# Single-core transformer stack: uniform widths in runs of full-precision products, rearranged last norm, and 18 added products in the feed-forward blocks

## What is computed

```python
def second_block(x, ...):
    h = x
    for l in range(DEPTH_2):                      # DEPTH_2 is 1
        h = h + 0.5 * swiglu(rmsnorm_2(h, ffn1_norm[l]), ffn1_w_gate[l], ffn1_w_up[l], ffn1_w_down[l])
        n = rmsnorm_2(h, mix_norm[l])
        ...                                       # block attention, spatial gating, sigmoid gates
        h = h + merged @ w_out[l]
        h = h + 0.5 * swiglu(rmsnorm_2(h, ffn2_norm[l]), ffn2_w_gate[l], ffn2_w_up[l], ffn2_w_down[l])
    return rmsnorm_2(h, final_norm)
```

## Time and profile before

| | |
|---|---|
| median of 3 runs | 1138.66 us (1137.09 to 1138.79) |
| profiled execution, its own time | 1136.31 us |
| its span in the profile | 1134.5 us |
| granted TensorE clock, mean | 0.998 |
| PE busy | 1120.8 us, 99% of the span |
| DVE / ACT / POOL busy | 733.8 / 653.8 / 750.8 us |
| chain that ended last, PE's share | 96% |

### The profile page before, as it was taken

How to read it: one execution, slowest core, us unless ns; L and a number is a source line. 1 busy time by engine, 2 the same in 40 slices (tenths; PEclk the granted TensorE clock), 3 DMA queues, 4 the chain that set the end, 5 groups by cost and what they waited for, 6 DMA issues and landing times.

```text
span 1134.5 us, 22331 instructions
## 1 busy us (share of the span) xinstructions
PE 1120.8 (99%) x8968; PEld 1066.2 (94%) x8968; DVE 733.8 (65%) x1261; ACT 653.8 (58%) x1089; POOL 750.8 (66%) x578
## 2 busy tenths in 40 slices
PE   9999999999999999999999999999999999999996
PEld 7788998999988799899999999999899999999996
DVE  6896644566588775265847666667669567666664
ACT  7676854575567577346646444446566447444443
POOL 6787697657488868865764656556865774646552
PEclk9999999999999999999999999999999999999999
DMA  9554354556555534545566566655644655566551
GB/s 319 181 179 130 119 182 151 171 161 205 168 168 169 168 120 151 184 139 180 169 215 202 188 221 188 198 179 178 207 148 131 205 188 166 189 217 191 192 180 38
DMA packets 63895, 199.49 MB, mean 176 GB/s; under 512 B 6992, under 2 KB 17968, under 8 KB 63792
## 3 DMA queue, kind: packets, MB, share of 16 engines
q1 hardware_dynamic: 61920, 194.99, 53.2%
q10 hardware_dynamic: 1872, 3.08, 0.8%
HBM read 196.21 MB, written 1.84 MB: 175 GB/s over the span
## 4 chain that ended last, share of the span: by engine, by line
PE 96%; DMA 1%; DVE 1%; issue 0%; ACT 0%; SPq 0%; DVEq 0%
PE ps L1665 51%; PE ps L1735 20%; PE ps L1725 14%; PE ps L1701 2%; PE ps L1893 2%; DMA par<-in_par 1%; PE ps L1987 1%; PE ps L1967 1%; PE ps L1997 1%; PE ps L1928 1%; PE ps L1988 0%; PE ps L1867 0%; PE ps L1954 0%; PE ps L1970 0%; PE ps L1845 0%
## 5 line engine op out<-in xcount | busy, mean ns | idle before, releaser
L368 POOL TENSOR_TENSOR ring<-raw,ring 128x512 fp32r<-128x512 f32 x516 | 717.8, 1397 | 358.1 <-ACT ring L483 337.0
L1665 PE MATMUL ps<-xs,ring 128*128 128x256 f32 x5040 | 598.0, 278 | 0.6 <-DVE mq L1019 0.6
L1665 PEld LDWEIGHTS ps<-xs,ring 128*128 128x128 f32 x5040 | 582.6, 188 | 5.1 <-issue 3.2
L483 ACT ACTIVATE ring<-raw 128x1024 fp32r<-128x1024 f32 x364 | 377.8, 1052 | 89.2 <-PE ps L1735 49.4
L1735 PE MATMUL ps<-ys,ring 128*128 128x256 f32 x2016 | 235.7, 276 | 0.2 <-DVE ys L1043 0.2
L1735 PEld LDWEIGHTS ps<-ys,ring 128*128 128x128 f32 x2016 | 231.7, 188 | 0.5 <-issue 0.3
L981 DVE TENSOR_TENSOR ring<-raw,ring 128x1024 fp32r<-128x1024 f32 x106 | 148.5, 1401 | 122.4 <-ACT ring L483 121.8
L1725 PE MATMUL ps<-ring,xs 128*128 128x512 f32 x672 | 164.5, 397 | 0.0
L1725 PEld LDWEIGHTS ps<-ring,xs 128*128 128x128 f32 x672 | 123.3, 188 | 26.6 <-issue 1.3
L812 ACT ACTIVATE ys<-ca 128x256 fp32r<-128x256 f32 x44 | 18.3, 416 | 94.2 <-DVE ca L1445 94.2
L1294 DVE SCALAR_TENSOR_TENSOR ca<-ps,par,ca 128x253 f32<-128x253 f32 (+2 forms) x96 | 45.9, 478 | 34.4 <-ACT ca L567 33.0
(11 more groups left out here) (274 smaller groups left out, 1011.8 us busy)
## 6 DMA issues: line engine op xcount, KB each, us to landing
raw<-in_w SPq DMA_DIRECT2D x364, 512.0 KB, 3.6
y<-bias_rows SPq DMA_DIRECT2D x6, 256.0 KB, 4.3
out_y<-y SPq DMA_DIRECT2D x4, 256.0 KB, 2.5
const<-in_const SPq DMA_DIRECT2D x1, 896.0 KB, 12.3
bias_rows<-lg ACTq DMA_DIRECT2D x1, 768.0 KB, 7.7
x<-in_x ACTq DMA_DIRECT2D x1, 512.0 KB, 4.3
x<-in_x SPq DMA_DIRECT2D x1, 512.0 KB, 6.8
dec<-in_wT ACTq DMA_DIRECT2D x1, 512.0 KB, 3.6
```

Source lines behind the costliest of these rows:

```text
L368: last = pool.tensor_tensor(ring[:, g % RING, 1, part], raw[:, g % RAW, part], ring[:, g % RING, 0, part].bitcast(F32), ALU.subtract)
L483: act.activation(ring[:, g % RING, 0, :], raw[:, g % RAW, :], ACT.Copy).then_inc(S["hi"], 1)
L1665: last = mm(ps[bank][:, half * T:(half + 1) * T], ring[:, slot % RING, wp, (at + k) * P:(at + k + 1) * P], rhs(k, xp), start=(first and i ...
```

## The change

Five things are changed.

1. In a mixer layer `index_columns` writes `ps[0]` and `forget_gate` writes `ps[1]`. `index_logits(0)` no longer waits for `iwT_ev` and `gl_x`; the first slot of R_DK, which writes banks 0 and 1 one slot later, waits for them.
2. Full-precision runs are put into products of 128 columns: `sum_squares` (2 of 256 become 4 of 128), `gla_squares` (2 of 512 become 8, and the job stands ahead of `dsa_turn(1)` rather than behind it), `ml_values` (256 and 128 become 3 of 128, three times a head), `scores2` (256 and 128 become 3 of 128).
3. In both feed-forward blocks three full-precision products (all-ones weights, identity as the moving operand, 128 columns each) stand ahead of the gate slot of tiles 4, 9 and 14. They write columns of the bank that the gate slot's first matmul then starts afresh.
4. In `tile(2)` of a feed-forward block ACT does its first split ahead of the tanh.
5. The end is rewritten: the last three sum slots are taken by output tile, so that banks close one after the other (`end_sums`); squares are partly added on DVE (`end_fold`); the sum over features has the squares as weights and one column of ones as the moving operand, which leaves 256 sums as a 128x2 tile; the inverse root is formed on that, and spread to all partitions by four products with the identity; ACT multiplies by the gains ahead of that (`end_gain`).

```diff
@@ SP @@
-            for k in range(0, KT, 2):
...
+            for k in (0, 2, 6, 4):
+                if k == 6:
+                    sp.wait_ge(S["last_f"], 1)
+                else:
                     sp.wait_ge(S["x_f"], FINAL_AT + k // 2 + 1)
@@ ACT @@
                 def tile(f):
                     p = at + 4 + 3 * (f - 2)
-                    gate_tanh(f)
-                    next_split(p)
+                    if f == 2:
+                        next_split(p)
+                        gate_tanh(f)
+                    else:
+                        gate_tanh(f)
+                        next_split(p)
                     product_hi(f)
...
+            end_square(0, 2)
+            end_square(2, 4)
+            for k in range(3):
+                end_gain(k)
+            end_square(4, 6)
+            end_square(6, 7)
+            end_square(7, 8)
+            for k in range(3, 5):
+                end_gain(k)
+            act.wait_ge(S["end_var"], 1)
+            step(act.activation(rms[:, 512:514], var[:, 0:2], ACT.Ln))
+            act.activation(rms[:, 512:514], rms[:, 512:514], ACT.Exp, scale=-0.5).then_inc(S["end_rms"], 1)
+            for k in range(5, 8):
+                end_gain(k)
+            act.wait_ge(S["end_ps"], 2)
+            act.activation(rms[:, 0:T], ps[6][:, 0:T], ACT.Copy).then_inc(S["end_sb"], 1)
@@ PE, sum_squares @@
                 for c in range(2):
-                    last = mm(ps[4][:, 0:T], ones, sqs[:, c * T:(c + 1) * T], start=(c == 0), stop=(c == 1))
+                    for a in (0, P):
+                        last = mm(ps[4][:, a:a + P], ones, sqs[:, c * T + a:c * T + a + P],
+                                  start=(c == 0 and a == 0), stop=(c == 1 and a == P), skip_group_check=True)
@@ PE, index_logits @@
                     if p == 0:
-                        pe.wait_ge(S["iwT_ev"], it + 1)
-                        pe.wait_ge(S["gl_x"], it + 1)
+                        pe.wait_ge(S["x_hi"], it * KT + 4)
+                        pe.wait_ge(S["x_lo"], it * KT + 4)
@@ PE, slots of a layer @@
+                        if q == 0 and r == R_DK:
+                            pe.wait_ge(S["iwT_ev"], it + 1)
+                            pe.wait_ge(S["gl_x"], it + 1)
                         arrived(p)
@@ PE, ffn @@
                     here(slot)
+                    if f in (4, 9, 14):
+                        for q in range(3):
+                            mm(ps[2 * (f % 2)][:, q * P:(q + 1) * P], ones, ident, start=True, stop=True)
                     tile_product(2 * (f % 2), 0, slot, xs_part).then_inc(S["slots_used"], 1)
@@ PE, the end @@
+                for n in range(4):
+                    part(n, (0, 1))
+                here(slot + 2)
+                pe.wait_ge(S["y_lo"], y_done + first + 3)
+                for n in range(4):
+                    ins = part(n, (2,))
+                    if n % 2:
+                        ins.then_inc(S["end_out"], 1)
+                part(4, (0, 1, 2))
+                part(5, (0, 1, 2)).then_inc(S["end_out"], 1)
+                part(6, (0, 1, 2))
+                part(7, (0, 1, 2)).then_inc(S["end_out"], 1)
...
+                    last = mm(ps[4][:, c:c + 1], sqs[:, k * T + c * P:k * T + (c + 1) * P], ones[:, 0:1],
+                              start=(first and c == 0), stop=(final and c == 1), skip_group_check=True)
...
+            for b in (5, 6):
+                for c in range(2):
+                    last = mm(ps[b][:, c * P:(c + 1) * P], rms[:, 512 + c:513 + c].broadcast_to((P, P)), ident,
+                              start=True, stop=True)
+                last.then_inc(S["end_ps"], 1)
```

More of the change, by code:

```diff
@@ L483, in split, with squares @@
                 act.activation(ring[:, g % RING, 0, :], raw[:, g % RAW, :], ACT.Copy).then_inc(S["hi"], 1)
-            def squares(n, last=False):
+            def squares(n):
                 for b in range(4):
                     act.wait_ge(S["x_new"], n * N_UPDATES + (b + 1))
-                    act.activation(ps[3][:, :] if b == 0 and not last else sqs[:, b * 512:(b + 1) * 512],
+                    act.activation(ps[3][:, :] if b == 0 else sqs[:, b * 512:(b + 1) * 512],
                                    x[:, 2 * b:2 * b + 2, :].rearrange("p a t -> p (a t)"), ACT.Square)\
@@ L842, in ffn @@
                     early(n + 1, par2, U_MIX)
-                squares(n + 1, last)
-                if not last:
+                    squares(n + 1)
                     for p in range(at + FFN_SLOTS - 2, at + FFN_SLOTS):
@@ L1802, in index_columns @@
                     pe.wait_ge(S["rest_in"], 16)
+                    pe.wait_ge(S["early"], it * EARLY + 5)
                     for tt in range(2):
-                        last = mm(ps[4][:, 8 * tt:8 * tt + 8], rows[:, tt * P:(tt + 1) * P], ident[:, 96:104],
+                        last = mm(ps[0][:, 8 * tt:8 * tt + 8], rows[:, tt * P:(tt + 1) * P], ident[:, 96:104],
                                   start=True, stop=True)
@@ L1849, in forget_gate @@
                     pe.wait_ge(S["wa_in"], 16 * it + 16)
+                    pe.wait_ge(S["early"], it * EARLY + 6)
                     for c in range(2):
-                        last = mm(ps[5][:, c * T:(c + 1) * T], wa[:, c * P:(c + 1) * P], rows, start=True, stop=True)
+                        last = mm(ps[1][:, c * T:(c + 1) * T], wa[:, c * P:(c + 1) * P], rows, start=True, stop=True)
                     last.then_inc(S["gl_ps"], 1)
@@ L1912, in gla_squares @@
                     for c in range(2):
-                        last = mm(ps[6 + c][:, :], ones, sqs[:, c * 512:(c + 1) * 512],
-                                  start=True, stop=True)
+                        for a in range(0, 512, P):
+                            last = mm(ps[6 + c][:, a:a + P], ones, sqs[:, c * 512 + a:c * 512 + a + P],
+                                      start=True, stop=True)
                     last.then_inc(S["gssq"], 1)
@@ L2058, in here, with end_sums, part, ffn @@
                 pe.wait_ge(lo[n % RAW], n // RAW + 1)
-            def ffn(at, n, h_done, y_done):
+            def end_sums(slot, y_done):
+                first = FFN_TILES - 3
+                def part(n, tiles):
+                    for i in tiles:
+                        for j, (wp, xp) in enumerate(PARTS):
+                            ins = mm(ps[4 + n // 2][:, n % 2 * T:(n % 2 + 1) * T],
+                                     ring[:, (slot + i) % RING, wp, n * P:(n + 1) * P], ys[:, (first + i) % YS, xp, :],
+                                     start=False, stop=(i == 2 and j == 2), skip_group_check=True)
+                    return ins
+                here(slot + 1)
+                pe.wait_ge(S["y_lo"], y_done + first + 2)
+                for n in range(4):
[10 more added lines that the diff above has]
+                part(7, (0, 1, 2)).then_inc(S["end_out"], 1)
+            def ffn(at, n, h_done, y_done, last=False):
                 here(at)
@@ L2083, in ffn @@
                         pe.wait_ge(S["y_lo"], y_done + 1)
-                    sum_slot(slot + 2, (f - 2) % YS, f == 2, False)
+                    if not last or f < FFN_TILES - 1:
+                        sum_slot(slot + 2, (f - 2) % YS, f == 2, False)
+                if last:
+                    end_sums(at + FFN_SLOTS - 3, y_done)
+                    return
                 for f in range(FFN_TILES - 2, FFN_TILES):
@@ L2101, in scores2 @@
                     pe.wait_ge(S["a_max"], h - 1)
-                mm(ps[4 + h % 2][:, P:3 * P], mq[:, h, P:T], dqk[:, 4 + h // 2, :], start=True, stop=True)
-                mm(ps[4 + h % 2][:, 0:P], mq[:, h, 0:P], dqk[:, 4 + h // 2, 0:P],
-                   start=True, stop=True).then_inc(S["a_ps"], 1)
+                for at, q, k in ((0, 0, 0), (P, P, 0), (2 * P, P, P)):
+                    last = mm(ps[4 + h % 2][:, at:at + P], mq[:, h, q:q + P], dqk[:, 4 + h // 2, k:k + P],
+                              start=True, stop=True)
+                last.then_inc(S["a_ps"], 1)
             def turn2(h):
```

86 lines of the change are left out of this document (56 added, 30 removed).

## The result

| | before | after |
|---|---|---|
| median | 1137.13 us (6 runs, 1136.25 to 1138.79) | 1141.62 us (6 runs, 1140.49 to 1143.19) |
| profiled execution, span | 1136.31 us, 1134.5 us | 1143.19 us, 1141.4 us |
| ratio of the medians | | 1.0038, 95% interval 1.0025 to 1.0051 |

A forecast was written before the change was run, and what follows sets the result against it. PE, busy 99% of the span, was taken to bound the kernel. The terms +4.2 - 2.0 - 0.3 + 0.3 - 2.7 gave -0.5 us, from 1138.66 to 1138.2 us, range 1134.8 to 1141.8 us.

The forecast's parts named there:

- 128 columns instead of 256 or 512: Re-cut full-precision runs: longer products, less slow pace behind six slots, net +0.3 us, ends -0.2 and +1.0.
- the runs of 128 alone that I found are followed by 2.74 or 2.75: Slots behind runs of only 128 columns were said to take 2.74 or 2.75 us, against 2.83 at the slow pace.
- Three added products, six times: Feed-forward blocks: each added group costs 0.70 us of PE time, six cost +4.2 us.
- No row offers anything in return: Feed-forward blocks: PE already at 113.3 ns a matmul, so the added products were expected to gain nothing.
- Index wait: Mixer layers: PE's 1.01 us stand ahead of the first index product goes, -2.0 us for both layers.
- ACT's order: Tile 2, feed-forward block 1: the earlier split removes PE's 0.27 us stand at a sum slot, -0.3 us.
- The six slow slots: One slot behind `gla_squares` in each layer and four behind `scores2`, at 2.83 us: -0.5 us if they settle.
- The end: Rewritten end: last sum slot to end of span in about 9.7 us instead of 12.4, -2.7 us.
- The sum: Whole kernel: all terms together -0.5 us, 1138.2 us, a difference not to be seen; chance 0.53.
- the first: Rival: the added products leave PE at the slow pace in both feed-forward blocks, 12.3 us, 1150.5 us; chance 0.11.
- The second rival: Unprofiled executions are partly at the slow pace, the products end it: 2.35 us gone, 1135.8 us; chance 0.18.
- The chance for slower by over 0.2%: Whole kernel: 0.18 for slower by over 0.2%, against 0.58 for within 0.2% and 0.24 for faster.

The follow-up runs named there:

- experiment 1: Changed kernel without the added groups: 1145.67 us; with the old widths: 1136.61 us; with both edits: 1137.49 us.
- Experiment 4: Changed kernel with old `sum_squares` alone: 1139.56 us; with old `ml_values` alone: 1138.34 us; with ten products a run in `ml_values`: 1141.12 us.
- experiment 5: Kernel before with only the six groups of three products added: 1141.68 us, ratio 1.0026 to the kernel before.
- experiment 6: Changed kernel, old widths, five extra products at the end: 1138.37 us; same, but groups only in block 2, ahead of tiles 3, 4, 5: 1140.32 us.
- no-groups: Changed kernel without the six groups of added products: 1145.67 us, ratio 1.0071 to the kernel before.
- four-a-group: Changed kernel with the old widths and four added products a group instead of three: 1144.80 us in one run.
- two-group kernel: Changed kernel with the old widths and two groups of three products a block, ahead of tiles 4 and 6: 1135.50 us, ratio 0.9972.
- the filler: Five 128-column products behind the end's one-column products, added to the changed kernel with old widths: 1138.37 us, ratio 0.9994 to the kernel before.
- third kernel of experiment 1: Changed kernel without the groups and with the old widths: 1137.49 us, ratio 0.9987 to the kernel before.
- experiment 2: Kernel before with 1 to 19 products of 128 columns ahead of gate slots and two of 256 ahead of up slots: profiled span 1244.5 us.
- experiment 3: Changed kernel with five products instead of four in `sum_squares`: 1140.12 us; with old widths and four products a group: 1144.80 us.

## Why the prediction was wrong

The step that failed is "128 columns instead of 256 or 512", put at +0.3 us; the runs showed +5.0 (experiment 1). Its own terms, the products, were about right. What failed is the sentence under it, that "the runs of 128 alone that I found are followed by 2.74 or 2.75", from which it put the slow pace behind such runs at nothing. I had found runs of 12 and 6 products in the layers, and took the width for the cause. The four-product run that the change makes of `sum_squares` and the nine-product run of `ml_values` are of neither count. Experiment 4 prices them: 3.3 us for `ml_values`, 2.1 for `sum_squares`, together about what all widths cost (5.0). For `sum_squares` the count is shown to be the cause; for `ml_values` the runs show that it is these products, and not why.

The trace of before already spoke against the width. The slot at 831.40 us, with its 2.74 us, stands right behind a run that mixes widths (its chain of waits):

```profile
830.75 0.43 PE ps L2122 x2
831.18 0.22 PE ps L2123 x2
831.40 2.74 PE ps L1665 x24
```

So fast slots stood behind both kinds of run, and that the slow ones were "all behind runs that mix widths" did not make the width their cause.

Step by step:

- *Three added products, six times, +4.2*: right for their own time in the profiles, 0.685 instead of 0.70 each; over executions of the kernel before they measured about 3.0 us (experiment 5). "No row offers anything in return" was wrong in two ways: the return was a slow pace that the change itself makes, and perhaps one that the profiled execution of before did not have and others of its runs did.
- *Index wait, -2.0*: right, -2.1.
- *ACT's order, -0.3*: PE has no stand at the second sum slot in the changed kernel (627.80 to 630.63 is 2.83, its slow pace exactly), so -0.3 there. Without a group ahead of tile 4 a stand of 0.2 us turns up one tile later (experiment 6): with the split first, the stand moved on rather than went.
- *The six slow slots, -0.5 if they settle*: the four behind `scores2` stayed slow (2.91 us each, with the gap to the next run); the two behind `gla_squares` settled (layer 0: 124.04 to 126.87 us, 2.83 with its longer first gaps).
- *The end, -2.7*: -1.8 in the profile. The forecast of 9.7 us from last sum to end of span is what profiles at full clock show (9.7 in the no-groups, the four-a-group and the two-group kernel); the changed kernel's 10.6 is the clock at half speed in the eight records of 128 columns (2.08 us for 1.16), a thing that the prediction did not have.
- *The sum*: against the profiled execution -0.5 was forecast and +6.9 came. Of the 7.4 between them the slow pace is 6.7 and the end 0.9; the small rest went the other way.

Of the rivals, the first named the right mechanism, a slow pace of long duration, but put it in the wrong place (behind the groups) and gave it 0.11. In the changed profile one of six groups was followed by a slow stretch, and it had come in slow. The second rival, unprofiled executions with slow blocks, may be true of some runs of before, but the 2.35 us on which it rested were mostly the small number of runs: with six the median of before was 1137.13 beside the changed kernel. The chance for slower by over 0.2% was 0.18; the range ended at 1141.8, just above the 1141.62 measured. That the time lies inside is luck: the edge allowed for the slow pace in one or two stretches behind the groups, and it came behind other products.

## What to carry to other kernels

A stream of matmuls may have two stable paces, as here, and a short run of other products or a short stand of PE can decide which one it keeps for the next hundred microseconds; read the start-to-start time of a slot in every long stretch, and compare kernels over many executions, since one profile shows only one of them. Before you re-cut products to another width, ask what count that gives next to a long stream, because the 2 to 6 us behind a run outweigh its own hundredths. One run of three products early in each block went with the lowest median here, and each further one cost its own time.

## What the runs showed of the hardware

- A stream of weight loads and 256-column matmuls kept either 113.3 or 117.8 ns a matmul for as long as 1500 matmuls (all of block 2 in the third kernel of experiment 1). The granted clock is 1.00 in both. The slow pace carries over to other widths: behind the slow stretch of layer 1 in the changed kernel the next 24 matmuls, of 512 columns, take 233.4 ns each (324.01 to 329.62 us), and 228.8 in the kernel before. The Trainium skill, "TensorE: Matmul & The Clock Gate", section "Back-to-back issue gap", says that in a stream of weight loads and matmuls the spacing is set by both. For an isolated matmul of 256 columns it lists 262 cycles, 109.2 ns at 2.4 GHz. Both paces of the runs lie above that figure.
- In the feed-forward blocks an even number of full-precision products of 128 columns turned the pace over and an odd number kept it, 38 of 38 in the one profile of experiment 2. Out of the fast pace this held at the sums and groups of every other profile too (experiment 3). Out of the slow pace it did not: at the sums and groups of the other fifteen profiles three products turned it fast in four of five cases (two in the changed kernel, one each in those with old and with ten-product `ml_values`), four in seven of nine, and two products of 256 columns in 11 of 13, though experiment 2 has three, and two of 256, keep it. What differs inside such a slow stretch stays open, and so does the cause of the two paces. The layers follow the rule only in part (experiment 4), and in the mixing stage three products of `scores2` behind three transposes leave a slot slow that was fast ahead of them (839.07 us, changed kernel).
- A short stand of PE in the middle of such a stream can turn the pace, and at the same place it does so in some executions and not in others. Ahead of block 2 all sixteen profiles have one start-to-start time of 448 to 455 ns among those of 113; behind it nine run at the slow pace and seven at the fast one. The seven meet a second of 197 to 206 ns; three of them go slow there. So block 2 is entered slow in twelve of sixteen. In block 1 a stand of 0.2 us left the pace fast in one profile and slow in another (experiment 6).
- The granted clock fell from 1.00 to 0.50 in the last microseconds in seven of eleven profiles of the new end without the filler, in part of the eight records in one more, and once in two with it, within a microsecond or two behind the sixteen one-column records. It costs 0.9 us. Whether the one-column products or something else bring it about was not settled.
